# A fused decoder-like kernel on one core: tap sums and block sums of the feed-forward kept in PSUM, one set of product banks, and another order of forming the first operands

## The reference, cut to what matters

```python
def conv_glu_ffn(h, w_up, conv_w, conv_b, w_down):
    a = h @ w_up                       # 1024 -> 2 * 2816
    a1 = jnp.pad(a, ((0, 0), (1, 0), (0, 0)))[:, :S]
    a2 = jnp.pad(a, ((0, 0), (2, 0), (0, 0)))[:, :S]
    c = conv_w[0] * a2 + conv_w[1] * a1 + conv_w[2] * a + conv_b
    gate, val = jnp.split(c, 2, axis=-1)
    return (jax.nn.silu(gate) * val) @ w_down
x = x + conv_glu_ffn(rmsnorm(x, ffn_norm_g), w_up, conv_w, conv_b, w_down)
```

## Time and profile before

| | before |
|---|---|
| median of 3 runs | 2803.94 us |
| the profiled execution's own time | 2803.27 us |
| its span, first to last instruction | 2801.5 us |
| PE busy | 2715.8 us, 97% |
| DVE busy | 1596.3 us, 57% |
| ACT busy | 1054.3 us, 38% |
| POOL busy | 1257.8 us, 45% |

### The profile page before, as it was taken

The page is one execution under the profiler, slowest core; times in us unless marked ns, Lnnn a source line. Parts: engine busy times, 40 slices in busy tenths (PEclk is TensorE's granted clock), DMA queues, the critical chain, the costliest instruction groups (busy, mean ns, idle before and its releaser), DMA issues.

```text
span 2801.5 us, 34490 instructions
## 1 busy us (share of the span) xinstructions
PE 2715.8 (97%) x13574; PEld 2188.7 (78%) x13574; DVE 1596.3 (57%) x2014; ACT 1054.3 (38%) x1598; POOL 1257.8 (45%) x625
## 2 busy tenths in 40 slices
PE   8999999998999999899999999999998999999998
PEld 6888887776877777788878888888876777777776
DVE  7335652238899999723266666666635444444455
ACT  5322222324444444312144554444524333333342
POOL 4333353125899999543322222222335333333335
PEclk9999999999999999999999999999998999999999
DMA  4012331002222222454322222222222111111114
GB/s 150 32 45 75 106 105 39 31 31 98 76 75 68 88 71 68 160 193 143 120 77 76 67 70 64 64 71 67 66 100 83 39 38 38 38 38 38 38 53 161
DMA packets 111785, 214.21 MB, mean 76 GB/s; under 512 B 32032, under 2 KB 61888, under 8 KB 111504
## 3 DMA queue, kind: packets, MB, share of 16 engines
q1 hardware_dynamic: 104992, 190.02, 20.8%
q10 hardware_dynamic: 6192, 20.18, 2.0%
q0 software_dynamic: 448, 1.88, 0.2%
HBM read 177.38 MB, written 34.67 MB: 76 GB/s over the span
## 4 chain that ended last, share of the span: by engine, by line
PE 73%; POOL 13%; DVE 6%; issue 4%; ACT 2%; DMA 1%; SPq 0%; ACTq 0%; POOLq 0%; DVEq 0%
PE gemm L973 16%; PE gemm L974 15%; PE gemm L975 15%; PE small L1155 2%; POOL raw_r L876 2%; PE small L1668 2%; PE small L1690 2%; POOL wlo_f L887 2%; PE small L973 2%; PE small L975 2%; PE small L974 2%; POOL pair_ex L876 2%; POOL w_lo L876 1%; PE small L1678 1%; POOL v_val_r L876 1%
## 5 line engine op out<-in xcount | busy, mean ns | idle before, releaser
L973 PE MATMUL gemm<-h_hi,w_hi 128*128 128x512 f32 x1988 | 851.2, 428 | 37.9 <-POOL raw_r L876 11.2
L974 PE MATMUL gemm<-h_lo,w_hi 128*128 128x512 f32 x1988 | 787.9, 396 | 0.0
L787 POOL TENSOR_TENSOR w_hi<-w_raw,unit_col 128x1024 fp32r<-128x1024 f32 x134 | 262.8, 1961 | 1133.8 <-PE gemm L975 881.7
L975 PE MATMUL gemm<-h_hi,w_lo 128*128 128x512 f32 x1900 | 751.9, 396 | 0.0
L973 PEld LDWEIGHTS gemm<-h_hi,w_hi 128*128 128x128 f32 x1988 | 376.9, 190 | 123.9 <-issue 16.1
L974 PEld LDWEIGHTS gemm<-h_lo,w_hi 128*128 128x128 f32 x1988 | 377.5, 190 | 72.8 <-issue 6.2
L975 PEld LDWEIGHTS gemm<-h_hi,w_lo 128*128 128x128 f32 x1900 | 357.8, 188 | 86.6
L796 POOL TENSOR_TENSOR w_lo<-w_raw,w_hi 128x1024 fp32r<-128x1024 f32 x118 | 305.7, 2590 | 13.8 <-DVE w_lo L2800 4.9
L2984 DVE SCALAR_TENSOR_TENSOR taps<-norm,vec,taps 128x1024 f32<-128x1024 f32 x88 | 190.8, 2187 | 29.7 <-ACT taps L2166 28.9
L934 POOL TENSOR_TENSOR w_hi<-w_raw,unit_col 128x1024 fp32r<-128x1024 f32 x32 | 60.6, 1895 | 324.7 <-PE gemm L975 324.7
L3002 DVE TENSOR_TENSOR t_lo<-t_lo_f,t_hi 128x1024 fp32r<-128x1024 f32 x40 | 50.9, 1314 | 142.8 <-ACT t_hi L2178 142.8
(11 more groups left out here) (549 smaller groups left out, 5588.2 us busy)
## 6 DMA issues: line engine op xcount, KB each, us to landing
w_raw<-w_stream SPq DMA_DIRECT2D x178, 512.0 KB, 3.5
t_lo_f<-act_spill SPq DMA_DIRECT2D x40, 512.0 KB, 4.4
act_spill<-taps SPq DMA_DIRECT2D x22, 512.0 KB, 2.9
x_spill<-xres ACTq DMA_DIRECT2D x16, 512.0 KB, 2.6
v_gate<-w_stream SPq DMA_DIRECT2D x11, 512.0 KB, 4.1
v_val<-w_stream SPq DMA_DIRECT2D x11, 512.0 KB, 3.4
xres<-x_t SPq DMA_DIRECT2D x8, 512.0 KB, 8.0
xres<-x_t ACTq DMA_DIRECT2D x8, 512.0 KB, 4.9
```

What stands on the lines that cost most here:

```text
L787: nc.gpsimd.tensor_tensor(whi[d][:, :, :], raw[s][:, :, :], unit, ALU.mult).then_inc(w_hi_done, 1)
L973: mm(dst, w_hi, a_hi, start=first, stop=False, skip_group_check=onto)
L974: mm(dst, w_hi, a_lo, start=False, stop=False, skip_group_check=onto)
L975: return mm(dst, w_lo, a_hi, start=False, stop=last, skip_group_check=onto)
```

## The change

1. One set of banks. All pairs now use `gemm0` and `gemm1`, as four half banks a, b, c, d. The two `small` banks hold the tap sums of gate and value for all pairs but the last (`tap_sum`).
2. DVE's sums are made in place in PSUM: `b` takes `SNAP1` and `SNAP5`, `c` and `d` take `U2`. `U2` is now ACT's copy of `b` (`u2_copy`), and the third snapshot is gone.
3. What PE waits for at the start of a product changes with the banks: the first product waits for the first scaled half of the gate (`ff_out`), the second for the second half (`ff_scaled`), the third for the scaled value tile (`ff_scaled`), all of the pair before.
4. At the start: T1's differences lie in `norm` and are made tile by tile, squares go to PSUM, the first slabs are split right behind tile 6, three wide splits (`b2_low`) come ahead of tile 7's addition, the root stands ahead of two high parts on ACT, and `spread` stands one product later on PE.
5. At the end, `ring_low(0)` stands ahead of the gate's sums of the last pair.

```diff
+        UP_BANKS = (gp[0][:, 0:HALF], gp[1][:, HALF:], gp[0][:, HALF:], gp[1][:, 0:HALF])
+        def tap_sum(p, v):
+            return ps[v][:, :] if p < PAIRS - 1 else taps[:, 2 * (p % 2) + v, :]
@@ squares
+            if j == NFF:
+                return ps[k % 2][:, :]
@@ up_product, PE
-                if j < 3 and p >= 2:
-                    pe.wait_ge(*ff_out(4 * (p - 2) + j + 2))
-                if p == 0 and j < 2:
-                    pe.wait_ge(tile_added, 2 * KT - 1 + j)
+                if p == 0 and j in (0, 2):
+                    pe.wait_ge(tile_added, 2 * KT - 1 + j // 2)
+                if p and j == 0:
+                    pe.wait_ge(*ff_out(3 * p))
+                if p and j in (1, 2):
+                    pe.wait_ge(*ff_scaled(2 * (p - 1) + j))
...
-                    if p == 0 and j == 3:
+                    if p == 0 and j == 4:
                         pe.wait_ge(norm_rstd, S_FF + 1)
                         spread(pa, R_H).then_inc(norm_wide, 1)
@@ the down projection, PE
-                    if e == 0 and q % 2 == 0:
-                        pe.wait_ge(*ff_out(4 * (PAIRS - 1 + q // 2)))
+                    if e == 0 and q < 2:
+                        pe.wait_ge(*ff_scaled(2 * (PAIRS - 1) + q + 1))
@@ ACT
+            def u2_copy(p):
+                act.wait_ge(*ff_out(3 * p + 2))
+                if p:
+                    act.wait_ge(*ff_scaled(2 * p))
+                A(U2, UP_BANKS[1], ACT.Copy).then_inc(snap.sem, 1)
...
-                A(taps[:, 2 * (p % 2) + v, :], Nf[...], ACT.Identity, ...)
+                A(tap_sum(p, v), Nf[...], ACT.Identity, ...)
@@ up_sums, DVE
-                done(V.tensor_tensor(SNAP5, SNAP5, SNAP7, ALU.add))
-                V.tensor_tensor(u2[:, :], bank[1], SNAP1, ALU.add).then_inc(ff_out.sem, 1)
-                done(V.tensor_tensor(a[:, 2 + HALF:], u2[:, :], SNAP5, ALU.add))
+                V.tensor_tensor(SNAP5, d, SNAP5, ALU.add).then_inc(ff_out.sem, 1)
+                V.tensor_tensor(b, b, SNAP1, ALU.add).then_inc(ff_out.sem, 1)
@@ up_gate, DVE (second half)
-                V.tensor_tensor(a[:, 2 + HALF:], bank[2], u2[:, :], ALU.add).then_inc(ff_out.sem, 1)
-                V.tensor_tensor(a[:, 2 + HALF:], a[:, 2 + HALF:], WIDE_FF[:, half(1)], ALU.mult).then_inc(ff_scaled.sem, 1)
+                done(V.tensor_tensor(c, c, U2, ALU.add))
+                V.tensor_tensor(Nf[:, 2 + HALF:2 + S], c, WIDE_FF[:, half(1)], ALU.mult).then_inc(ff_scaled.sem, 1)
@@ up_value, DVE
-                V.tensor_tensor(a[:, 2:2 + HALF], bank[3], u2[:, :], ALU.add).then_inc(ff_out.sem, 1)
-                V.tensor_tensor(a[:, 2:], a[:, 2:], WIDE_FF, ALU.mult).then_inc(ff_scaled.sem, 1)
+                done(V.tensor_tensor(d, d, U2, ALU.add))
+                done(V.tensor_tensor(b, b, SNAP5, ALU.add))
+                V.tensor_tensor(Nf[:, FP + 2:2 * FP], gp[1][:, :], WIDE_FF, ALU.mult).then_inc(ff_scaled.sem, 1)
@@ the last pair, DVE
                 up_sums(p)
-                up_gate(p)
                 if p == PAIRS - 1:
                     ring_low(0)
-                up_gate_late(p)
+                up_gate(p)
```

More of the change, by code:

```diff
@@ L228, in build @@
         hhi = sb("h_hi", [P, KT, S], F32R)
-        with nc.sbuf_tensor("h_lo_f", [P, KT, S], F32) as hlo_f:
-            pass
         hlo = sb("h_lo", [P, KT, S], F32R)
@@ L2162, in tap2 @@
                     act.wait_ge(*t4_ready(KT // 2))
-                if p >= 2:
-                    act.wait_ge(act_stored[p % 2], 16 * (p // 2)) if v == 0 else act.wait_ge(ff_prod, p - 1)
+                if p == PAIRS - 1:
+                    if v == 0:
+                        act.wait_ge(act_stored[p % 2], 16 * (p // 2))
+                elif p:
+                    act.wait_ge(ff_gate, p) if v == 0 else act.wait_ge(ff_prod, p)
                 q = 2 * p + v
-                A(taps[:, 2 * (p % 2) + v, :], Nf[:, v * FP + 2:v * FP + 2 + S], ACT.Identity, bias=vc("ff_b", q),
+                A(tap_sum(p, v), Nf[:, v * FP + 2:v * FP + 2 + S], ACT.Identity, bias=vc("ff_b", q),
                   scale=vc("ff_w", 2 * 2 * PAIRS + q)).then_inc(ff_tap2.sem, 1)
@@ L2170, in gate @@
                 act.wait_ge(ff_conv, p + 1)
-                A(taps[:, 2 * (p % 2), :], taps[:, 2 * (p % 2), :], ACT.Silu).then_inc(ff_gate, 1)
+                if 2 <= p < PAIRS - 1:
+                    act.wait_ge(act_stored[p % 2], 16 * (p // 2))
+                A(taps[:, 2 * (p % 2), :], tap_sum(p, 0), ACT.Silu).then_inc(ff_gate, 1)
             def ring_high_part(j):
@@ L2186, in _ @@
                     tap2(p - 1, 1)
+                    gate(p - 1)
                 snapshot(p, 1)
-                if p:
-                    gate(p - 1)
-                snapshot(p, 2)
                 if p == 0:
@@ L2197, in _ @@
                     high_s2(p + 1)
+                u2_copy(p)
+                if more:
                     high_a12(p + 1)
@@ L2919, in _ @@
                     for n in range(3):
+                        t_diff(m - 4, n)
+                    for n in range(3):
                         t_low(m - 4, n)
@@ L2922, in _ @@
                     add_square(NFF, m)
+                if m == KT - 2:
+                    for k in range(4, KT - 1):
+                        b2_low(k)
+            add_square(NFF, KT - 2)
             for n in range(3):
                 t_diff(3, n)
-            add_square(NFF, KT - 2)
             t_low(3, 0)
@@ L2993, in product @@
                 dve.wait_ge(ff_gate, p + 1)
-                gate, value = taps[:, 2 * (p % 2), :], taps[:, 2 * (p % 2) + 1, :]
-                V.tensor_tensor(gate, gate, value, ALU.mult).then_inc(ff_prod, 1)
+                gate = taps[:, 2 * (p % 2), :]
+                V.tensor_tensor(gate, gate, tap_sum(p, 1), ALU.mult).then_inc(ff_prod, 1)
             def ring_low(j):
```

95 lines of the change are left out of this document (40 added, 55 removed).

## The result

The median went from 2803.79 us (4 runs, 2803.15 to 2806.31) to 2768.99 us (4 runs, 2767.70 to 2769.71): a ratio of 0.987, 95% interval 0.986 to 0.989. The profiled execution took 2768.67 us, with a span of 2766.9 us against 2801.5. The forecast was 2766, its range 2757 to 2781.

The account below looks back on a forecast made before the run. POOL, held up by DVE instructions with two SBUF inputs, was taken to bound pairs 1 to 20. Gains of 25.3 (pairs), 7.0 (start) and 6.3 (end), 38.6 us, took the profiled 2803.27 to 2764.7, median forecast 2766, range 2757 to 2781.

Parts of the forecast that it names:

- What bounds the kernel: Pairs 1 to 20: POOL's 11 instructions bind at 21.02 us a pair; PE has 1.48 us to spare.
- Pairs 1 to 20: Middle pairs: POOL's relief leaves PE the bound at 19.54 us a pair, a gain of 25.3 us.
- The row of a later stage: Later-stage SCALAR_TENSOR_TENSOR with one SBUF and one PSUM input: 1.29 us with POOL idle or busy, taken for the new tap.
- The tightest place: Next pair's third product, bank d: scaling ends at 23.5 us, product starts at 25.1, 1.6 us to spare.
- The rival with 0.5 to 1 us a pair: Third product waits 0.5 to 1 us in each pair behind a longer seven-step chain: 2776 to 2786 us; 10%.
- the slower one: Rival: the chain to the third product becomes the pair's bound, 23.5 us a pair, 2845 us in all; 3%.
- The surcharge for a PSUM source: DVE instructions reading PSUM: the skill's 65 ns more each would leave the third product 1.2 us of spare.
- The two rules: DVE operands: the contention rule favours at most one SBUF input beside GpSimd; the PSUM surcharge speaks against moving operands there.
- The start: Pair 0: first products need only tile 6, third waits 5 us for tile 7; pair 1 starts 7.0 us earlier.
- The end: Down projection's first 24 matmuls: 2.4 us lost at the value tile in place of 8.7, a gain of 6.3.
- The sum: Whole kernel: 25.3 + 7.0 + 6.3 = 38.6 us gained, forecast 2766 us.
- Everything behind moves up as a whole: Behind the feed-forward: all waits on PE or on what PE releases, so it moves up as a whole.

Follow-up runs that it names:

- The execution with 1.95 us for `token_sums` and 4.41 for the fourth product: Changed kernel plus two DVE multiplications a pair with both inputs in SBUF, output to a buffer nothing reads; 2765.60 us.

## Why the prediction was right, point by point

- *What bounds the kernel.* Right. A pair takes what the larger of PE's 19.54 us and POOL's eleven instructions asks for. POOL's mean over its eleven instructions (from the groups by form, 712 to 1085 us) was 1.91 us before, 1.63 with the tap sums in SBUF, 1.48 before without taps, 1.40 with the two added instructions, 1.33 with the value summed in SBUF and 1.29 after, and only with the first, 21.0 us a pair, is it above PE.
- *Pairs 1 to 20: 25.3 us.* Measured 25.3. DVE's tap 1.29 us as forecast, POOL 11 x 1.29 = 14.2 us, PE at 19.54. The row of a later stage stood for the new form rightly.
- *The tightest place, 1.6 us of spare at the third product.* Measured 1.67, and tested with 1.47 us more on the chain. The rival with 0.5 to 1 us a pair, and the slower one, had the right place, and each needed a chain that is longer than it was.
- *The surcharge for a PSUM source,* which the Trainium skill ("VectorE: DVE Perf Modes", the section on the TRN2 errata) states, doesn't show: two adds of 512 columns with one PSUM input (L2977 and L2979) take 0.69 us each and start 0.60 us apart in the kernel after; those with both inputs in SBUF (L2914) take 0.68 to 0.69 us and start 0.60 apart as well. The 0.62 us of the prediction was 2.49 / 4, the span of four over four; between their starts lie three steps. The two rules point opposite ways here, and the contention is the one that counts.
- *The start: 7.0 us forecast, 5.3 measured.* Tile 7 was added at 681.96 (forecast 682.0), the third product began at 682.06 (682.1) after a stop of 5.1 us (5), `token_sums` at 688.15 (688.7). The step that failed comes next: "`token_sums` 2.0 (as long as L1135) until 690.7; fourth product until 693.5". It took 3.09 us, and the fourth product from 691.1 to 696.0, its matmuls 0.63 us long and not 0.39. I had let the clock come back after twelve matmuls, as the rows of before showed it for the stop at 681.01; here it was back at 685.2, after seven, was lower again in the sixteen tiny matmuls behind the next short wait, and stayed so for ten of the fourth product's twelve. Together these took 2.95 + 4.90 us where the sum had 2.0 + 2.8; `spread`, 0.8 us and not 1.6, and `token_sums`' start gave 1.35 us back. The trace of before had the hint: six of its own fourth product's matmuls ran at the lower level, behind no long stop:

```profile
692.27 0.42 PE L975 MATMUL gemm<-t_hi,pair_ex 128*128 128x512 f32 x1
692.50 0.62 PE L973 MATMUL gemm<-t_hi,w_hi 128*128 128x512 f32 x1
```

The execution with 1.95 us for `token_sums` and 4.41 for the fourth product shows the same step at its cheaper price, 703.86.
- *Whose gain it was.* The prediction worked out the start as one sum and credited the order. By the experiments some 3.6 of the 5.3 us are there without the order; the squares' 2.3 us are shown, the banks' part is not shown apart from the clock's. Both were in my sum (squares at 1.2 us, first products without tile 7), only not named as parts.
- *The end: 6.3 forecast, 3.6 measured.* The place was right, the wait too (2.72 us at the value tile, forecast 2.4). What was mis-sized is what lies beside it: the low parts of the ring took DVE from 1111.66 to 1114.0, pushing the gate's sums, so that the tap ended at E + 3.7 (E is the pair's end, 1115.63) and not E + 2.6, and the scaling at E + 6.2 and not E + 5.2; and the clock fell, nine matmuls in 3.74 us for 2.10, 1.6 us. My sum had this only in its bound ("the wait is 4 us and the clock falls"). The low parts were late because what they read was: DVE stood for ACT's high parts, and ACT for the stored result that is read back from DRAM.

```profile
1111.66 2.36 DVE L3008 TENSOR_TENSOR t_lo<-t_lo_f,t_hi 128x1024 fp32r<-128x1024 f32 x2 [3.45 <-ACT t_hi L2193]
1110.57 2.01 ACT L2193 ACTIVATE t_hi<-t_lo_f 128x1024 fp32r<-128x1024 f32 x2 [1.73 <-DMA t_lo_f<-act_spill]
```

The ring's new place ahead of the gate's sums was not run by itself. The kernel before without taps lost nothing at the end with the ring in its old place, so DVE being ahead of PE is enough there.
- *The sum.* 34.2 of the 38.6 us came, and the median lies 3 us above the forecast of 2766. The pairs' 25.3 us were met, the start fell short by 1.7 us and the end by 2.7; neither miss hid the other, though within the start `spread`'s lower price hid a part of the fourth product's.
- *Everything behind moves up as a whole.* Right within the scatter of 2 us given above.

## What to carry to other kernels

Two engines that slow each other down show as one of them with a mean duration that varies from group to group for the same instruction; compare the durations of one form before counting instructions, and move one input of the *other* engine's work to PSUM. The gain stops where the next engine binds: the block sums in PSUM would have been enough for the pairs here, and the tap sums bought nothing more there. Where an engine stands still for some microseconds, count the clock's slow matmuls behind the stop into the price, and ask first whether the operand that is late must be asked for so early: turning the order of four banks gave 5.1 us, the reordering at the start 1.3 to 3.1.

## What the runs showed of the hardware

- The price of a meeting is paid on both sides. A DVE instruction of 128x1024 with two SBUF inputs goes from 1.22 to 2.2 us beside POOL's work, POOL's 128x512 from 1.29 to between 2.0 and 2.3. The instruction that comes into the other engine's waits for its end: 1.55 us for the one of POOL that started 0.38 us before the end of DVE's, 2.20 us for the next one of DVE. In the kernel before, too, the ends lie in turn: POOL's (from 878.68) at 880.84, DVE's (L2975, from 880.38) at 881.92, POOL's next (from 880.81) at 883.10.
- Sixteen matmuls with one column (`token_sums`) took 1.95, 2.25, 2.98, 3.09, 3.41 and 3.57 us in runs of nearly the same start, by how much of them ran at the clock's lower level: the granted clock of these stretches was 1.00, 0.85, 0.62, 0.60, 0.50 and 0.50 (1.00 is 2.4 GHz, 0.50 is 1.2 GHz). With the same code, pair 1 started between 703.86 and 705.62 us; a stretch behind a stop of some microseconds varies by that much from one execution to the next.
